# First layer of a two-layer decoder step on one core: another order of stages inside each gap, top-256 rounds and selected softmax at other places, a third load buffer

## What is computed

```python
z = rmsnorm(x, pre_w) @ w_in            # 3652 columns: qa ka va ga | qb kb vb gb | qi ki wi
# A: differential attention, 4 heads of 2 x 64
attn = p[:, :, 0] - lam * p[:, :, 1]    # "combine" in the kernel, gives "diffs"
oa = rmsnorm(attn @ v) * (1 - lam_init) # "a_norm"
# B: the index scores choose the keys, 256 of 1025 for a sample, 64 of 256 for a prompt token
score = sum_h wi * relu(qi . ki);  _, sel = top_k(score, n_keep)
ob = softmax(qb . kb[sel]) @ vb[sel]
mix = concat(oa * silu(ga), ob * silu(gb));  y = x + rmsnorm(mix @ w_out, post_w)
```

## Time and profile before

| | |
|---|---|
| median of 3 runs | 1023.43 us (1023.19 to 1025.41) |
| the profiled execution | 1027.02 us, of it 1025.2 us span |
| mean granted clock of TensorE | 0.881 |
| PE busy | 847.6 us (83%), 4952 instructions |
| PEld busy | 443.6 us (43%) |
| DVE busy | 435.3 us (42%) |
| ACT busy | 244.0 us (24%) |
| POOL busy | 161.3 us (16%) |
| moved by DMA | 213.99 MB, mean 209 GB/s |

### The profile page before, as it was taken

How to read it: one execution, slowest core, us unless ns; L and a number is a source line. 1 busy time by engine, 2 the same in 40 slices (tenths; PEclk the granted TensorE clock), 3 DMA queues, 4 the chain that set the end, 5 groups by cost and what they waited for, 6 DMA issues and landing times.

```text
span 1025.2 us, 12847 instructions
## 1 busy us (share of the span) xinstructions
PE 847.6 (83%) x4952; PEld 443.6 (43%) x4952; DVE 435.3 (42%) x965; ACT 244.0 (24%) x591; POOL 161.3 (16%) x204
## 2 busy tenths in 40 slices
PE   3989796676798779778675898789999999899894
PEld 2545444233344333333243454355555444455552
DVE  2214248677556439534622512422453513342214
ACT  2333112212121420113111412223321122233112
POOL 0230301110101123224030101261312000000000
PEclk9989788788799879979796899999989798999887
DMA  7545727547454566747754658498879943823701
GB/s 247 202 133 199 256 79 262 213 136 289 154 212 127 169 237 212 243 127 276 293 194 176 241 177 277 152 378 320 325 275 366 334 179 108 290 83 100 253 10 43
DMA packets 68325, 213.99 MB, mean 209 GB/s; under 512 B 5056, under 2 KB 28784, under 8 KB 62888
## 3 DMA queue, kind: packets, MB, share of 16 engines
q0 software_dynamic: 20864, 142.55, 38.4%
q1 hardware_dynamic: 47400, 70.62, 20.1%
HBM read 207.11 MB, written 64.68 MB: 265 GB/s over the span
## 4 chain that ended last, share of the span: by engine, by line
PE 52%; DMA 7%; DVE 6%; ACT 4%; issue 3%; POOL 2%; ACTq 0%; DVEq 0%
PE psum L819 23%; PE psum L883 9%; PE psum L773 5%; PE psum L830 3%; DMA ring<-in_cache_a_v,index 3%; PE psum L970 2%; PE psum L1307 2%; PE psum L938 2%; DMA ring<-in_cache_b_v,index 1%; POOL ring L746 1%; DMA ring<-in_cache_c_cmp_v,index 1%; PE psum L1209 1%; PE psum L1243 1%; PE psum L1149 1%; DMA ring<-in_state_c_win_v 1%
## 5 line engine op out<-in xcount | busy, mean ns | idle before, releaser
L819 PE MATMUL psum<-ring,XB 128*128 128x512 f32 (+3 forms) x832 | 380.0, 614 | 7.0 <-DMA ring<-in_w_in_even 2.8
L819 PEld LDWEIGHTS psum<-ring,XB 128*128 128x128 f32 x832 | 167.8, 207 | 193.9 <-issue 185.6
L883 PE MATMUL psum<-Z,ring 128*128 128x512 f32 x256 | 123.8, 630 | 0.0
L1777 DVE TENSOR_TENSOR RT<-Z,const 128x128 f32<-128x128 f32 (+6 forms) x43 | 11.5, 267 | 187.4 <-ACT Z L1451 169.9
L883 PEld LDWEIGHTS psum<-Z,ring 128*128 128x128 f32 x256 | 49.3, 201 | 66.4 <-issue 65.3
L1451 ACT COPY Z<-psum 128x512 f32<-128x512 f32 (+3 forms) x38 | 20.3, 534 | 205.2 <-PE psum L819 205.1
L773 PE MATMUL psum<-const,ring 128*128 128x128 f32 (+1 forms) x288 | 46.6, 311 | 21.8 <-DMA ring<-in_cache_b_idx,index 8.9
L1377 ACT COPY NW<-psum 128x512 f32<-128x512 f32 (+1 forms) x56 | 32.7, 584 | 89.2 <-PE psum L773 88.2
L1588 ACT ACTIVATE SM<-SM,stat 128x128 f32<-128x128 f32 (+4 forms) x56 | 26.8, 479 | 113.5 <-DVE stat L1943 112.6
L773 PEld LDWEIGHTS psum<-const,ring 128*128 128x128 f32 (+1 forms) x288 | 35.1, 150 | 39.5 <-issue 13.3
L830 PE MATMUL psum<-ring,XB 128*8 128x128 f32 (+3 forms) x1664 | 50.6, 277 | 1.3 <-ACT XB L1377 1.3
(11 more groups left out here) (316 smaller groups left out, 922.5 us busy)
## 6 DMA issues: line engine op xcount, KB each, us to landing
ring<-in_w_in_odd SPq DMA_DIRECT2D x9, 2048.0 KB, 9.7
ring<-in_w_in_even SPq DMA_DIRECT2D x6, 2048.0 KB, 9.7
ring<-in_cmp_w SPq DMA_DIRECT2D x4, 2048.0 KB, 8.5
ring<-in_w_in_odd SPq DMA_DIRECT2D x8, 1024.0 KB, 7.3
out_s_d_k<-in_state_d_k POOLq DMA_DIRECT2D x8, 1022.0 KB, 7.2
out_s_d_v<-in_state_d_v POOLq DMA_DIRECT2D x8, 1022.0 KB, 9.3
ring<-in_w_out_even SPq DMA_DIRECT2D x2, 2048.0 KB, 15.3
Z<-in_cmp_w POOLq DMA_DIRECT2D x4, 1024.0 KB, 7.4
```

The source lines that it names most:

```text
L819: last = mm(out[:, 0:n], xT[:, k, t * 128:(t + 1) * 128], w[:, k * n:(k + 1) * n], start=k == 0, stop=k == KT - 1)
L883: last = mm(out[:, h * 512:(h + 1) * 512], w[:, (r % 16) * CH + h * 128:(r % 16) * CH + h * 128 + 128], rowsT[:, at:at + 512], start=r == ...
```

## The change

Nothing is computed otherwise, and the number of instructions of each kind stays as it is. What changes is order and place:

- gaps 0 to 15: a `prep` stands ahead of the gap's `rows`, and output, probs and scores of a gap stand ahead of the rest of it; `index_sum(1)` moves to gap 12, and gap 12 has no `top`;
- gaps 16 to 31: `probs(7)`, `output(7)`, `scores(8)` and `probs(8)` move one gap or a place on; `a_scores` stands ahead of `a_norm(0)`; four `top` rounds stand in gaps 27, 29, 30 and 31; `a_turn` stands behind `cache(1, 0)`;
- a `top` round stands behind each `cache(1, b)`, and the first `a_values` behind b = 2, 4, 6; the second compression has 16 rounds where it had 24, and `kept` stands in its last step, where three more rounds stood behind `gelu(1, 0)`;
- `own_mask`, `mask_keys` and `soft("b")` stand ahead of the first `out_rows`; `second(1, 1)` ahead of the third; `norm_y(0, 0)` ahead of the fourth, `xn(1, 0)` and `norm_y(0, 1)` ahead of `turn_mix(0, 2)`;
- loads: `probs` is open to all items, and a new home `heads` (2048 columns of QK) is open from `scores(11)` to `soft("b")`; A's softmax rows move from QK to SM for that, and the squares of some norms go to a scratch in Z;
- copies: none after the first three `bv`, twelve after the last;
- second layer: `prep` ahead of `rows`; `second_prompt(0)`, `key_prompt` and `second_prompt(1)` one gap on.

```diff
--- before.py
+++ after.py
@@ -218,33 +218,36 @@
             5: [("head_weights",), ("cache", 0, 6), keys[1], ("cache", 0, 7)] + product(),
             6: keys[2:3] + [("index_turn",)] + keys[3:4] + product(),
             7: keys[4:5] + [("index_scores",)] + keys[5:6],
-            8: keys[6:7] + [("prep", 0, 0), ("own_a",), ("top_prompt", 4)] + product(),
+            8: keys[6:7] + [("own_a",), ("top_prompt", 4)] + product(),
             9: keys[7:8] + [("top_prompt", 4)] + product(),
-            10: keys[8:9] + [("prep", 0, 1), ("top_prompt", 4)] + product(),
-            11: [("index_sum", 0), ("index_sum", 1), ("top_prompt", 4)] + product(),
-            12: [("prep", 0, 2), ("top_mask",), ("top", 1)] + product(),
+            10: keys[8:9] + [("top_prompt", 4)] + product(),
+            11: [("index_sum", 0), ("top_prompt", 4)] + product(),
+            12: [("index_sum", 1), ("top_mask",)] + product(),
             13: [("top", 1)] + product(),
-            14: [("prep", 0, 3), ("top", 1)] + product(),
+            14: [("top", 1)] + product(),
             15: [("top", 1)] + product()}
+    preps = {8: 0, 10: 1, 12: 2, 14: 3}
     starts = {8 + u: u for u in range(8)}
     for gap in range(16):
         i, t = gap // 2, gap % 2
+        if gap in preps:
+            order.append(("prep", 0, preps[gap]))
         order.append(("rows", 0, i, t))
         if t and i:
             order.append(("decode_rows", 0, i))
         if gap - 1 in starts:
             order.append(("combine", starts[gap - 1]))
+        units_at(order, gap, starts)
         order += gaps.get(gap, [])
-        units_at(order, gap, starts)
-
-    first = {16: [("combine", 7), ("output", 6), ("probs", 7)] + product(),
-             17: [("query", "b"), ("output", 7)],
-             18: [("own", "b")] + product(), 19: [("prep", 0, 4), ("prep", 0, 5), ("scores", 8)],
-             20: product(), 21: [("probs", 8), ("prep", 0, 6), ("scores", 9)], 22: product(),
+
+    first = {16: [("combine", 7), ("output", 6)] + product(),
+             17: [("query", "b"), ("probs", 7)],
+             18: [("own", "b"), ("output", 7)] + product(), 19: [("prep", 0, 4), ("prep", 0, 5)],
+             20: [("scores", 8)] + product(), 21: [("prep", 0, 6), ("probs", 8), ("scores", 9)], 22: product(),
              23: [("output", 8), ("probs", 9), ("scores", 10)], 24: product(),
              25: [("output", 9), ("probs", 10), ("scores", 11)], 26: product(),
-             27: [("output", 10), ("probs", 11)], 28: [("output", 11), ("a_norm", 0)], 29: [("a_scores",)],
-             30: [("a_norm", 1)], 31: [("a_turn",)]}
+             27: [("output", 10), ("probs", 11), ("top", 1)], 28: [("output", 11), ("a_scores",)],
+             29: [("a_norm", 0), ("top", 1)], 30: [("a_norm", 1), ("top", 1)], 31: [("top", 1)]}
     steps = [("compress", 0, r) for r in BLK_ORDER]
     for gap in range(16, 32):
         order += first.get(gap, [])
@@ -252,26 +255,29 @@
     order += [("gelu", 0, 0), ("top", 1)]
     values = [("a_values", b, half) for b in range(NB) for half in range(2)]
     for b in range(NB):
-        order += [("cache", 1, b)] + ([values.pop(0)] if b in (3, 5, 7) else [])
+        order += [("cache", 1, b), ("top", 1)] + ([("a_turn",)] if b == 0 else [])
+        order += [values.pop(0)] if b in (2, 4, 6) else []
     order += [("gelu", 0, 1)]
     steps = [("compress", 1, r) for r in BLK_ORDER]
     keys = [("keys", "b", s) for s in range(TILES["b"] + 1)]
     side = {7: [("second", 0, 0)], 8: [("second", 0, 1)], 10: [("kc_turn",)], 12: [("turn_mix", 0, 0)],
             13: [("spread", "a")], 14: [("turn_mix", 0, 1), ("a_norm", 2)]}
+    tops = [2, 1, 1] + [1] * 12
     for i in range(16):
         for j in (0, 1):
             order.append(steps[2 * i + j])
             if i >= 7 and j:
                 order.append(keys.pop(0))
-        order += [("top", 2 if i % 2 == 0 else 1)] + ([values.pop(0)] if values else []) + side.get(i, [])
+        order += ([("top", tops[i])] if i < len(tops) else [("kept",)]) + ([values.pop(0)] if values else [])
+        order += side.get(i, [])
     assert not keys
-    order += [("gelu", 1, 0), ("top", 3), ("kept",)]
-    order += [("out_rows", 0, 0, 0), ("own_mask",), ("mask_keys", 0), ("mask_keys", 1), ("soft", "b"), ("gelu", 1, 1),
-              ("out_rows", 0, 0, 1), ("turn", "b"), ("second", 1, 0), ("values", "b", 0), ("values", "b", 1),
-              ("out_rows", 0, 1, 0), ("second", 1, 1), ("values", "b", 2), ("values", "b", 3), ("out_rows", 0, 1, 1),
-              ("spread", "b"), ("norm_y", 0, 0), ("turn_mix", 0, 2), ("norm_y", 0, 1),
-              ("out_decode_rows", 0, 0), ("xn", 1, 0), ("out_decode_rows", 0, 1), ("turn_x", 1, 0), ("xn", 1, 1),
+    order += [("gelu", 1, 0), ("own_mask",), ("mask_keys", 0), ("mask_keys", 1), ("soft", "b"), ("out_rows", 0, 0, 0),
+              ("gelu", 1, 1), ("turn", "b"), ("out_rows", 0, 0, 1), ("second", 1, 0), ("values", "b", 0),
+              ("values", "b", 1), ("second", 1, 1), ("out_rows", 0, 1, 0), ("values", "b", 2), ("values", "b", 3),
+              ("norm_y", 0, 0), ("out_rows", 0, 1, 1), ("spread", "b"), ("xn", 1, 0), ("norm_y", 0, 1),
+              ("turn_mix", 0, 2), ("out_decode_rows", 0, 0), ("out_decode_rows", 0, 1), ("turn_x", 1, 0), ("xn", 1, 1),
               ("norm_y", 0, 2)]
+    assert sum(e[1] for e in order if e[0] == "top") == TOPK_S // 8
     return order
 
 
@@ -285,8 +291,8 @@
             21: (1, 1), 22: (1, 0), 24: (1, 0), 25: (1, 0), 26: (1, 1), 27: (2, 2), 28: (2, 0)}
     extra = {1: [("turn_x", 1, 2), ("decode_rows", 1, 0)],
              4: [("fold_in",), ("fold", 0, 0)], 5: [("fold", 0, 1)], 6: [("hidden", 0)],
-             7: [("second_prompt", 0), ("fold", 1, 0)], 8: [("key_prompt",), ("fold", 1, 1)], 9: [("hidden", 1)],
-             10: [("second_prompt", 1)], 12: [("score_d", 0, 0)], 14: [("score_d", 0, 1)], 16: [("score_d", 1, 0)],
+             7: [("fold", 1, 0)], 8: [("second_prompt", 0), ("fold", 1, 1)], 9: [("key_prompt",), ("hidden", 1)],
+             11: [("second_prompt", 1)], 12: [("score_d", 0, 0)], 14: [("score_d", 0, 1)], 16: [("score_d", 1, 0)],
              17: [("score_d", 1, 1)], 20: [("score_d", 2, 0)], 21: [("score_d", 2, 1)]}
     starts = {5: 12, 6: 13, 7: 14, 8: 15, 9: 16, 10: 17, 11: 18, 12: 19, 13: 20, 14: 21}
     starts.update({20 + i: 22 + i for i in range(8)})
@@ -297,10 +303,10 @@
         if i <= LAST[1]:
             if gap == 1:
                 order += [("turn_x", 1, 1), ("xn", 1, 2)]
+            order += [("prep", 1, k) for k in preps.get(gap, ())]
             order.append(("rows", 1, i, t))
             if t and i:
                 order.append(("decode_rows", 1, i))
-        order += [("prep", 1, k) for k in preps.get(gap, ())]
         early, late = take.get(gap, (0, 0))
         decode(order, dec, early)
         order += extra.get(gap, [])
...
@@ -557,7 +565,9 @@
         homes = [dict(slot="rows0", view=ring[:, 4 * PART:5 * PART], span=(0, len(ORDER)), before=[], only=None),
                  dict(slot="rows1", view=ring[:, 5 * PART:6 * PART], span=(0, len(ORDER)), before=[], only=None),
                  dict(slot="probs", view=PD[:, :], span=(step_of["turn_x", 0, 2], step_of["a_scores",]),
-                      before=["turn_x0"], only="score_a")]
+                      before=["turn_x0"], only=None),
+                 dict(slot="heads", view=flat[:, 1024:3072], span=(step_of["scores", 11], step_of["soft", "b"]),
+                      before=["heads_read"], only=None)]
         homes += [dict(slot=f"late{t}", view=late[t], span=(step_of["norm_y", 0, 2], step_of["rows", 1, 10, 0]),
                        before=["z_free", "outs0"], only=None) for t in (0, 1)]
         spare_from = step_of["decode_rows", 1, LAST[1] - 1]
@@ -722,7 +732,7 @@
                          moved("d_k1", 512) + moved("d_v1", 512), moved("c_win_k", 128) + moved("c_win_v", 128)):
             MOVES += group
 
-        MOVED_AFTER = dict(ak=1, bv=4, ck=2, cv=2, dk=2, wk=2, wv=2)
+        MOVED_AFTER = dict(ak=1, ck=2, cv=2, dk=2, wk=2, wv=2)
 
         def stream(eng, name, parts):
             slot, before = place[name]
@@ -940,6 +950,8 @@
                 mark(("softened", n), S.free, S.made)
                 for d in u["deps"]:
                     mark(("qk", d), S.full, S.made)
+                if n == 11:
+                    release("heads_read", S.full, S.made)
 
             def probs(n):
 
...
@@ -1382,10 +1394,10 @@
                 return T.reading
 
 
-            def norm(t, src):
+            def norm(t, src, scratch):
 
                 n = TOK[t][1]
-                act(PD[0:n, 1024:2048], src[0:n], ACT.Square, accum_out=stat[0:n, 60 + t:61 + t])\
+                act(scratch[0:n], src[0:n], ACT.Square, accum_out=stat[0:n, 60 + t:61 + t])\
                     .then_inc(sem("squares"), 1)
                 eng.wait_ge(sem("squares"), count(sem("squares")))
```

(5 more changed lines are left out.)

16 lines of the change are left out of this document (9 added, 7 removed).

## The result

The changed kernel took 1012.46 us (median of six, 1010.36 to 1016.92) beside 1024.42 us of the kernel before: a ratio of 0.988, interval 0.985 to 0.992. It is faster, as forecast, but by 12 us and not by 62, and the time lies outside the range of 940 to 990. Run twice more on other chips it took 1003.79 and 1003.05 us, with ratios of 0.978 (0.972 to 0.983) and 0.978 (0.974 to 0.981): about 24 us faster. What makes these pauses was not shown.

What follows compares the result with a forecast made beforehand. TensorE was taken to set the time, through its work and queue holes, each costing idle time and then half clock. Seven parts summed to -62 us, from 1023.4 to 961.4 us; forecast band 946 to 977, range 940 to 990.

Steps and rivals of the forecast that it cites:

- Part 1: 50 to 126.8 us: home probs open to all loads lets early gathers land sooner, closing two holes; -15 us.
- Part 2: Gaps 8 to 15: output, probs and scores right behind combine, long VectorE work under the next rows; -10 us.
- Part 3: Gaps 16 to 31: a_scores ahead of a_norm(0) shortens its wait, top rounds fit beside PE's work; -3.5 us.
- Part 4: Cache steps: gathers turn in the heads buffer, a_turn moves in behind top rounds; +2 us, bounds -3 and +8.
- Part 5: Second compression: three gather buffers close waits on in_cache_a_v and in_cache_b_k; -18 us, bounds -21 and -10.
- Part 6: End of first layer: kept earlier and copies behind bv_3 close holes, norm_y adds 1.8; -15.5 us.
- Part 7: Second layer: preps ahead of rows close some 1 us and may open one; -2 us, bounds -5 and +4.
- Step (b): From probs(1) to probs(2): VectorE's 14.8 us of work sets the length, 20.3 before; 5.1 us hole goes; -5.5 us.
- Step (c): Behind scores(7): compression starts 3.6 us after probs(6), where it took 14; -10.3 us.
- Step (a): Six gaps not set by VectorE: PE loses cover before combine, +1.0 to +2.0 us a gap, +8 in all.
- rival 2: Transfers become the limit: idxk1 late (+8), second compression buffers slow (+10), copies delay win1_0 (+5); 985 us, chance 0.13.
- Rival 4: Gaps 8 to 15: uncovered waits before probs keep the clock at half throughput, rows groups 11.5 us; 1042 us, chance 0.03.

Runs made afterwards that it cites:

- control: The changed kernel run again unchanged, on another chip, without the pauses: 1003.79 us, ratio 0.978 to the kernel before.
- first profile: Profile from the first measurement of the changed kernel, with pauses of PE inside decode_rows: 1012.46 us, ratio 0.988 to the kernel before.
- early_copies: Changed kernel with the old second-layer list, four top rounds moved from before a_turn into second compression, two copies per ak load, none behind bv_3: 977.17 us.
- second_alone: The kernel before with nothing but the new second-layer list, on a chip with pauses: 1034.21 us, ratio 1.007.
- cover: Changed kernel with keys, index sums and prep of gaps 8 to 15 placed between combine and probs: 1001.04 us, ratio 0.975.
- units_last: Changed kernel with output, probs and scores of a gap behind the rest of the gap again: 1002.36 us, ratio 0.976.
- index_back: Changed kernel with index_sum(1) back in gap 11, behind index_sum(0): 1002.62 us.
- after: The changed kernel as first measured and profiled, against the kernel before: 1012.46 us, ratio 0.988.
- free_turn: Changed kernel with four top rounds taken from in front of a_turn into steps 1 to 4 of the second compression: 992.34 us, ratio 0.967.
- heads_alone: The kernel before with only the home heads and what it needs, its own order and copies: 1002.06 us, ratio 0.976.
- late_copies: Changed kernel with the twelve copies behind bv_3 moved to the end of POOL's list: 1009.79 us, ratio 0.984.
- preps_back: Changed kernel with prep behind rows again in the second layer, second_prompt and key_prompt still one gap on: 1001.83 us, ratio 0.975.

## Why the prediction was wrong

By its parts, from the kernel before to control, the profile without pauses (spans 1025.2 and 1001.6):

| part | forecast | measured |
|---|---|---|
| 1, early gathers | -15 | -12.5 (first profile -5.2) |
| 2, gaps 8 to 15 | -10 | -9.5 |
| 3, gaps 16 to 31 | -3.5 | -0.6 |
| 4, cache steps | +2 | +10.7 |
| 5, second compression | -18 | -18.0 |
| 6, end of the first layer | -15.5 | -6.5 |
| 7, second layer | -2 | +12.8 |
| sum | -62 | -23.6 |

Parts 4, 6 and 7 make 32.5 of the 38 us that are missing, and each of them has an experiment that gives them back. With all three mended (early_copies, 977.17 us with the pauses in it) the ratio is 0.952; the forecast was 0.939.

**Part 1** was right in its mechanism: no wait on in_cache_b_idx. On the chips with pauses 7 us of it are lost. No row of before shows a pause: its decode_rows at 108.6 us runs through, and where second_alone has the pauses at the same place, a wait for the same gathers covers them.

**Part 2** came mostly as forecast, read from one probs to the next. Step (b), from probs(1) to probs(2), is 15.2 us (forecast 14.8, before 20.3). Step (c), from probs(6) to compression, is 4.3 us (forecast 3.6, before 14.0). Step (a), put at +8, is +8.2 in the other gaps, but 5.7 of that lie in the one gap that took over index_sum(1) (23.2 us for 17.5), and the lost cover itself can't be told from the scatter of cover and units_last. Two things were luck: the three terms give -7.8 and -10 was taken, and 2.9 us are gained ahead of probs(0), which no term has. Part of (b) was laid to the wrong edit: moving index_sum(1) gains nothing (index_back), the wait on KC goes because output stands ahead of the sums (units_last). The waits of 2.5 to 4.4 us before probs are near the 3 and 4.4 foreseen.

**Part 3**: the step that failed is "about 2 go" of the 3.3 us in a_scores. It waits 3.2 us still, for VectorE.

**Part 4** failed in one step, that VectorE starts a_turn 10.5 us after cache(1,0). It does so after 18 (346.09 - 328.12 us). The mistake is in part 3, "DVE has 28 us of work and PE 30" from the a_scores copies to the end of gap 31. VectorE takes 26 us there (in control from 304.4 to 330.3), near enough. PE has half of what I wrote, the four gaps in one row of after:

```profile
312.32 1.06 PE L783 MATMUL psum<-const,SA 128*64 128x128 f32 x4 [3.20 <-DVE SM L2231]
313.18 15.11 PE L893 MATMUL psum<-Z,ring 128*128 128x512 f32 x32
```

The rows of before had it: eight of these products take 3.70 us, so 32 take 15. So the rounds were not hidden, they queued in front of a_turn. free_turn shows it: 10.8 us back in D. The turns of the `heads` buffer, 2.7 us late each, were foreseen.

**Part 5** was followed load by load. Its mechanism is shown: the waits on in_cache_a_v and in_cache_b_k are gone, PE is busy 92.8 of 94.3 us, and heads_alone has the gain without the rest. That the sum came out to the tenth is luck, since it holds "less 2 to 3 for what I overlook" and an estimate of the clock. It carries the change.

**Part 6**: in the first profile -16.9 of the forecast -17.3 us had come by spread(b), with the waits named: 2.2 for kept, 8.0 for 8.3 before turn_mix. The step that failed is that the sum charges the twelve copies behind bv_3 nothing, though the load of win1_0 follows them. Without copies beside it that load is there 7.6 and 7.8 us after its issue (late_copies, early_copies), with them after 15.6 (527.15 to 542.77), and PE, which comes 2.8 us after the issue, waits for it. F is 9.7 us shorter in late_copies and 9 in early_copies, where it is 15.8 us below before, the forecast of this part. So "nothing is gained by that" held for the rest: the 2.6 us before turn_x are gone, and in early_copies 4.8 us on the load stand there instead. The delay by the copies was the third term of rival 2, put at 5 us with a chance of 0.13. The Trainium skill's page DMA: Bandwidth & Descriptors (Queues, rings and completion order) has a mechanism for it, engines turning between the queues that have work. The trace agrees that the load on SP's queue is slowed while POOL's copies run, 15.6 us for 7.6; it doesn't show the turning itself.

**Part 7** failed in sign. "Preps ahead of rows close some 1 us and may open one" had a bound of +4; it costs 12.2 us (preps_back), half in waits for ACT's copies and half in slower matmuls. I asked whether the ropes that prep needs are ready, and did not ask whether ACT could empty the two banks, right behind a softmax. The second half stays open.

Of the rivals, none was the case; 2 and 3 each have one term in it (win1_0, and the first a_values late for VectorE by 7.8 us where I wrote 14). Rival 4 did not happen: the clock rose from 0.77 to 0.80 in gaps 8 to 15. Of its signs, the projection groups of that stage take 7.03 to 9.81 us (one in control 10.19) and not 11. The rule that I cited beside it, from the Trainium skill's page TensorE: Matmul & The Clock Gate (HAM oscillation), shows in single groups, 7.03 us with no wait ahead and 8.07 behind a wait, but not as a clock lost throughout.

## What to carry to other kernels

Ask of a transpose which engine empties its bank, and what that engine has just been given: here it was a softmax, and the transposes were cheaper behind long matrix work than ahead of it. Before vector work is called hidden, count both engines' rows between the same two events; here 30 us were written where PE had 15. When a stage gets shorter, price the first load of the next one anew, and place bulk copies where no weights are waited for: between 110 and 301 us they cost nothing that could be seen, at the end of the layer or of the kernel 10 and 15 us.

## What was not expected of the hardware

The changed kernel has or lacks seven to ten pauses of PE, of up to 1.2 us, in its runs of 64 small matmuls while gathers are issued beside them. They begin after 39 to 49 matmuls of a run, and all kernels on a chip agree: some 4 us idle, and A 7 to 10 us longer. Comparisons of such kernels between chips are uncertain by that much.
